# First expert's token slots from one comparison pass, and the selection rounds moved between the weight splits of expert 0

## The reference

```python
aff = jax.nn.softmax((tok @ w_router).astype(jnp.float32), axis=-1)
cap = EC_CAPACITY_FACTOR * N // N_EXPERTS          # 64 of the 512 tokens of a group
gate, idx = lax.top_k(aff.T, cap)
xs = tok[idx]
hid = jax.nn.silu(jnp.einsum('ecd,edf->ecf', xs, w_exp_gate)) * jnp.einsum('ecd,edf->ecf', xs, w_exp_up)
out = jnp.einsum('ecf,efd->ecd', hid, w_exp_down) * gate[..., None].astype(h.dtype)
y = jnp.zeros((N, D), out.dtype).at[idx.reshape(-1)].add(out.reshape(-1, D))
```

## Time and profile before

| | us |
|---|---|
| median of three executions | 2386.59 (2385.63 to 2387.28) |
| the profiled execution, its own time | 2386.68 |
| span of its trace, first to last instruction | 2384.8 |
| TensorE busy in it | 2360.4 |
| VectorE, ScalarE, GpSimd busy | 1624.6, 1488.6, 401.4 |

### The profile page before, as it was taken

The page is one execution under the profiler, slowest core; times in us unless marked ns, Lnnn a source line. Parts: engine busy times, 40 slices in busy tenths (PEclk is TensorE's granted clock), DMA queues, the critical chain, the costliest instruction groups (busy, mean ns, idle before and its releaser), DMA issues.

```text
span 2384.8 us, 33778 instructions
## 1 busy us (share of the span) xinstructions
PE 2360.4 (99%) x11804; PEld 1967.3 (82%) x11804; DVE 1624.6 (68%) x1767; ACT 1488.6 (62%) x1707; POOL 401.4 (17%) x279
## 2 busy tenths in 40 slices
PE   8999999999999999999998999999999999999998
PEld 7888888888888888888885888888888888888886
DVE  5545464634546455455346988888888888888897
ACT  5656564533466465554335777777777777777776
POOL 1533433000053324320002000000000000000000
PEclk9999999999999999999999999999999999999999
DMA  6413321125432224112238999999999999999998
GB/s 189 128 45 100 88 73 67 70 98 204 158 98 83 83 62 126 64 63 80 90 155 334 403 393 382 383 383 381 390 387 393 387 383 383 385 387 376 394 375 326
DMA packets 214395, 557.35 MB, mean 234 GB/s; under 512 B 11968, under 2 KB 93376, under 8 KB 209216
## 3 DMA queue, kind: packets, MB, share of 16 engines
q1 hardware_dynamic: 207280, 530.89, 60.4%
q0 software_dynamic: 7056, 25.69, 3.6%
HBM read 533.47 MB, written 23.07 MB: 233 GB/s over the span
## 4 chain that ended last, share of the span: by engine, by line
PE 97%; DVE 1%; DMA 0%; issue 0%; ACT 0%; POOLq 0%; SPq 0%; DVEq 0%; ACTq 0%
PE bank L1433 44%; PE bank L1073 15%; PE bank L1118 13%; PE bank L1039 7%; PE bank L1062 5%; PE bank L1093 3%; PE bank L1236 2%; PE bank L1479 2%; PE bank L1134 2%; PE bank L1217 1%; PE bank L1156 1%; PE bank L1197 1%; PE bank L1203 1%; PE bank L1160 1%; PE bank L1252 0%
## 5 line engine op out<-in xcount | busy, mean ns | idle before, releaser
L2575 DVE TENSOR_TENSOR m_lo<-m_raw,m_hi 128x2048 fp32r<-128x2048 f32 x380 | 867.4, 2290 | 121.0 <-ACT m_hi L1925 117.4
L1925 ACT ACTIVATE m_hi<-m_raw 128x2048 fp32r<-128x2048 f32 x382 | 733.6, 1921 | 261.5 <-PE bank L1433 256.6
L1433 PE MATMUL bank<-m_hi,xs_hi 128*128 128x512 f32 x1032 | 321.0, 392 | 0.0
L1433 PE MATMUL bank<-m_hi,xs_lo 128*128 128x512 f32 x1032 | 317.9, 389 | 0.0
L1433 PE MATMUL bank<-m_lo,xs_hi 128*128 128x512 f32 x1032 | 317.8, 389 | 0.0
L2063 DVE TENSOR_TENSOR w_lo<-w_raw,w_hi 128x1152 fp32r<-128x1152 f32 (+4 forms) x110 | 145.0, 1344 | 180.1 <-ACT w_hi L1561 180.0
L1433 PEld LDWEIGHTS bank<-m_lo,xs_hi 128*128 128x128 f32 x1032 | 193.7, 188 | 40.5
L1433 PEld LDWEIGHTS bank<-m_hi,xs_lo 128*128 128x128 f32 x1032 | 193.7, 188 | 40.4
L1433 PEld LDWEIGHTS bank<-m_hi,xs_hi 128*128 128x128 f32 x1032 | 191.4, 188 | 38.2 <-DVE xs_lo L2597 0.2
L1073 PE MATMUL bank<-h_hi,w_hi 128*128 128x512 f32 x512 | 203.0, 396 | 0.0
L1073 PE MATMUL bank<-h_lo,w_hi 128*128 128x512 f32 x512 | 199.6, 390 | 0.0
(11 more groups left out here) (292 smaller groups left out, 4239.4 us busy)
## 6 DMA issues: line engine op xcount, KB each, us to landing
m_raw<-in_w_exp_gate SPq DMA_DIRECT2D x128, 1024.0 KB, 8.1
m_raw<-in_w_exp_up SPq DMA_DIRECT2D x128, 1024.0 KB, 7.6
m_raw<-in_w_exp_down SPq DMA_DIRECT2D x128, 1024.0 KB, 7.4
w_raw<-in_w_b SPq DMA_DIRECT2D x66, 512.0 KB, 6.2
w_raw<-in_w_a SPq DMA_DIRECT2D x24, 1024.0 KB, 5.1
w_raw<-in_w_c SPq DMA_DIRECT2D x24, 1024.0 KB, 4.8
w_raw<-in_w_d SPq DMA_DIRECT2D x8, 1024.0 KB, 6.5
xt<-in_x SPq DMA_DIRECT2D x8, 512.0 KB, 7.9
```

The costliest lines, as they stand in the source:

```text
L1433: mm = pe.matmul(ps[:, half, :], a[:, chunk + k, :], v[:, k, 512 * half:512 * (half + 1)], start=first and k == n == 0, stop=last and k == ...
L1925: act.activation(m_hi[slot.slot][:, :, :], m_raw[raw.slot][:, :, :], ACT.Copy)\
L2575: dve.tensor_tensor(m_lo[slot.slot][:, :, :], m_raw[raw.slot][:, :, :], m_hi[slot.slot][:, :, :].bitcast(F32), ALU.subtract)\
```

## The change

1. **First expert's slots.** For expert 0 alone the tokens are no longer taken from the selection rounds. The affinities of expert 0, multiplied by 2^64 (`raised`), are transposed onto all partitions, four tiles of 128 tokens for each group. VectorE then compares each tile with all tokens that can stand ahead of it (`compared`, four SCALAR_TENSOR_TENSOR instructions of 512, 384, 256 and 128 columns, each of which also sums its row), TensorE counts the other side of the comparisons, the difference of both is the token's rank, and an equality with a table of slot numbers marks its slot. TensorE picks token numbers and affinities with these marks. This is done for group 0 inside the closing schedule, for group 1 at its end. The table is loaded into a buffer that is free by then.
2. **The rounds.** The selection rounds, which still make the lists of experts 1 to 15, stand later on VectorE: rounds 0 to 2 while the first rows are gathered, rounds 3 to 5 behind the split of unit 10, rounds 6 and 7 and the merge behind that of unit 15. The filler that went with them is gone, and `WARM_GATHER` is 3 instead of 6.
3. **GpSimd** splits unit 0 alone, behind the issue of the first gather; units 1 and 2 go to VectorE, behind the split of the first rows.
4. **Loading.** SyncE issues three units, and the fourth waits for the rows of the first gather and for the picks. `final_gain` is loaded later.
5. **Order of expert 0.** All its gate and up columns come first (16 units), then all its down columns (8), then the first gate and up columns of expert 1. The loop covers experts 1 to 14.

The core of the diff:

```diff
-WARM_START, WARM_FIRST, WARM_GATHER, WARM_SPLIT, WARM_NORM = 3, 1, 6, 2, 4
-WARM_ROUNDS = {1: 1, 2: 1, 3: 1, 4: 1, 5: 1, 6: 1, 7: 1}
+WARM_START, WARM_FIRST, WARM_GATHER, WARM_SPLIT, WARM_NORM = 3, 1, 3, 2, 4
-EARLY_SPLITS = 2
+POOLED = (0,)
+RAISE = 2.0 ** 64
...
-                ("N", 3), ("k", 2), ("e", 0), ("l", 2), ("L", 3), ("E", 1), ("k", 3), ("e", 1), ("l", 3),
-                ("E", 2), ("E", 3), ("e", 2), ("b", 0), ("e", 3), ("B", 3)]
+                ("N", 3), ("k", 2), ("e", 0), ("l", 2), ("L", 3), ("t", 1, 0), ("E", 1), ("k", 3), ("e", 1), ("l", 3),
+                ("t", 1, 1), ("E", 2), ("E", 3), ("e", 2), ("t", 1, 2), ("e", 3), ("t", 1, 3), ("b", 0), ("B", 3), ("q", 0),
+                ("r", 1, 0), ("r", 1, 1), ("r", 1, 2), ("r", 1, 3), ("d", 3), ("c", 1), ("o", 1), ("q", 1), ("p", 1)]
...
-                if unit.k == RAW_SLOTS - 1:
+                if unit.k == 3:
 
                     sp.wait_ge(s_gather, 16)
+                    sp.wait_ge(s_picked, 2 * NB)
...
+            def compared(of, nth):
+
+                j, cols = NT - 1 - nth, P * (NT - nth)
...
+                dve.scalar_tensor_tensor(beats[j][:, :], ranked[of][:, 0:cols], raised[:, of, j:j + 1], margins[:, T - cols:],
+                                         ALU.subtract, ALU.is_gt, accum_out=row_sum[:, of, j:j + 1]).then_inc(s_beats, 1)
...
+            gate_cols()
+            hidden_transposes(1)
+            up_cols()
+            operand_ready()
+            lists_turned()
+            for j in range(4):
+                use(ps_d, hid_hi, hid_lo, MK * j, j == 0, False)
+                if j == 2:
+                    hidden_transposes(2)
+            operand_ready(1)
+            for j in range(4):
+                if j == 2:
+                    operand_ready()
+                use(ps_d, hid_hi, hid_lo, MK * j, False, j == 3)
+                if j == 2:
+                    token_transposes(32)
```

More of the change, by code:

```diff
@@ L602, in tile_read, with lo_ready @@
             eng.wait_ge(s_proj_free[proj.slot], START + proj.lap + 1)
+        def lo_ready(eng, unit, behind=0):
+            k = unit.k - behind
+            if k in POOLED:
+                eng.wait_ge(s_plo, POOLED.index(k) + 1)
+            else:
+                eng.wait_ge(s_mlo, unit.n(1 - behind - sum(each < k for each in POOLED)))
         def all_stored(eng, count):
@@ L990, in _ @@
             gather(1, 1)
-            with pool.Fori(0, NE - 2) as e:
+            pool.wait_ge(s_mtr, 8)
+            pool.wait_ge(s_gather, 32)
+            gather(2, 2)
+            add(0, 3)
+            with pool.Fori(1, NE - 2) as e:
                 pool.wait_ge(s_mtr, e * 6 + 6)
@@ L1310, in seam_step @@
                     pe.matmul(logits[i], parts[i % 2], fold[:, :], start=True, stop=True).then_inc(s_logit, 1)
+                elif what == "t":
+                    of = arg[0]
+                    if i == 0:
+                        all_read(pe, s_out_free, outs)
+                        all_read(pe, s_proj_free, proj, but=0 if of else 2)
+                    pe.wait_ge(s_raised, of * (1 + i) + 1)
+                    pe.transpose(ranked[of][:, natural(i)], raised[:, of, i:i + 1].to_broadcast([P, P]), ident[:, :])\
+                        .then_inc(s_rows, 1)
+                elif what == "c":
+                    if i == 0:
+                        all_read(pe, s_sc_free, sc)
+                    for j in range(NT - 1, 0, -1):
+                        pe.wait_ge(s_beats, i * NT + NT - j)
+                        for k in range(j):
+                            last = pe.matmul(counts[i], beats[j][:, natural(k)], unit_cols[:, k, :],
+                                             start=j == NT - 1 and k == 0, stop=j == 1)
+                    last.then_inc(s_counts, 1)
+                elif what == "q":
+                    pe.wait_ge(s_hot, 2 * i + 1)
+                    mine = slice(CAP * i, CAP * (i + 1))
+                    for k in range(NT):
+                        for part in range(2):
+                            last = pe.matmul(pick[mine, :], hot_16[:, i, k, :], tokens_16[:, i, k, part:part + 1],
+                                             start=k + part == 0, stop=k + part == NT)
+                    last.then_inc(s_picked, 1)
+                    pe.wait_ge(s_hot, 2 * i + 2)
+                    for k in range(NT):
+                        last = pe.matmul(pick_gate[mine, :], hot[:, i, k, :], raised[:, i, k:k + 1],
+                                         start=k == 0, stop=k == NT - 1)
+                    last.then_inc(s_picked, 1)
                 elif what == "b":
@@ L2039, in _ @@
             per = {"raw": 24, "slot": 24, "unit": 24, "done": 24, "tr": 6, "step": 2}
-            with rolled(act, NE - 1, mt, per) as e:
-                expert(e)
+            with rolled(act, NE - 2, mt, per) as e:
+                expert(e + 1)
             last_expert()
```

284 lines of the change are left out of this document (214 added, 70 removed).

## The result

The changed kernel takes 2391.61 us (median of 17 executions, 2389.16 to 2393.33), the kernel before 2386.52 (17, 2384.83 to 2388.47). The ratio is 1.0021 with a 95% interval of 1.0014 to 1.0027: 5.1 us slower, 6.5 us above the 2385.1 that I forecast and outside my range. The profiled execution of the changed kernel took 2389.88.

What follows compares the result with a forecast made beforehand. TensorE, busy 2360.4 of 2384.8 us, was taken as the bound. An earlier start of -9.0 and stalls of +7.2 gave -1.8, taken as -1.6 with small waits, from 2386.6: 2385.1 us, range 2381.2 to 2389.4.

Steps and rivals of the forecast that it cites:

- -9.0 for the start: First gather's rows land at 1275.4 instead of 1284.4, so expert work begins 9.0 us earlier, at 1278.3.
- +7.2 for the stalls: TensorE waits in expert 0: 3.3 us at unit 11, 1.5 at 16, 0.8 at 17 and 18 together, 1.6 at 20.
- 0.2 us for small waits: Waits of 0.04 us at each unit, counted to turn the sum of -1.8 into -1.6.
- The seam, +1.0: Ahead of the last norms, group 0's four transposes and six small matmuls on TensorE delay everything following by 1.0 us.
- The comparison chain: From last reciprocal at 1264.4 to gather issue at 1271.2; as rival, delayed to 1277.6, +4.8 us or more, 3 in 100.
- "It is not later than the issue": With three weight units beside it, the last store of rows lands no later than the gather's issue at 1271.2.
- The gather itself: The first gather takes 4.2 us (3.4 to 4.9) from issue to rows landed.
- The fourth unit: Issued when rows land, at 1275.4, it arrives 5.3 us later, then one unit per 2.56 us; split in time.
- both rivals on slow weights: Units come every 3.37 us behind the gather: five so, 2388.3 us (12 in 100); twelve or more, 2390.8 (8 in 100).
- "From unit 24 on everything stands as before.": After expert 0's units, the rest of the kernel was to run unchanged, at no cost.
- The clock: TensorE's raised clock might return 2 us late near the gather, moving the start 1 to 2 us.
- the cover of the rounds: Rival: VectorE builds full lead, stalls for rounds shrink from 4.8 to about 0.5 us; 2380.6 us, 17 in 100.

Runs made afterwards that it cites:

- Experiment 1: Changed kernel with the transposes of group 0's raised affinities one tile later in the closing schedule; 2390.33 us, kernel before 2386.75.
- Experiment 6: Changed kernel with weight units 1 and 2 issued only when the last normalised rows are stored; 2391.22 us, kernel before 2387.14.
- Experiment 2: Also written rounds_in_wait: changed kernel with rounds 3 and 4 moved into the gather wait, round 5 ahead of unit 8's split; 2386.58 us, kernel before 2386.75.
- Experiment 11: Idle two-column matmuls added ahead of the loop, 55 to the changed kernel, 64 to 512 to the kernel before; an iteration took 67.96 or 68.05 to 68.06 us.
- experiment 4: Also written filler_4: changed kernel with WARM_GATHER 4 instead of 3, one more filler in the gather wait; 2391.94 us, kernel before 2386.75.
- experiment 5: Changed kernel with the edits of Experiment 1 and Experiment 2 together; 2385.70 us, kernel before 2387.14.
- experiment 10: Kernel before with the fourth weight unit waiting for the first gather's rows and ScalarE's rounding of it behind xs_hi; 2390.37 us, unedited 2386.26.
- padded: Changed kernel with 55 two-column matmuls more behind the gather wait's filler, run once for the loop's pace; 68.05 us for an iteration.
- seven_units: Changed kernel with seven weight units issued ahead of the first gather and the eighth waiting for the rows; 2392.71 us, kernel before 2386.75.

## Why the prediction was wrong

By its own steps, in the order of the sum. The sum was -9.0 for the start and +7.2 for the stalls, -1.6 with 0.2 us for small waits; the profiled pair shows +3.3, and the medians +5.1.

- **The seam, +1.0.** It was +1.43 at the first addition behind the transposes (`xr` at 1233.00 for 1231.57 in the earlier trace rows), and 0.25 more behind the counts. The step counted instructions and left out that the transposes wait for VectorE's `raised`. Experiment 1 shows the wait and its size.
- **The comparison chain** came out at the right place, index at 1269.92 where I had 1270.2, but partly by luck: it began 0.5 us later than I had it (the last reciprocal at 1264.91 for 1264.4) and was 0.8 shorter from there, 5.0 us for 5.8. The four comparisons took 1.96 us where 1.6 had been counted in proportion to their columns. The small matmuls were cheap, as taken (eight picks and their latency 0.58 us), and VectorE's comparison of 512 columns took 0.75 where I had 0.69.
- **"It is not later than the issue"**, the last store of rows. This is the step that failed in the start: the store took 10.12 us with three units beside it, as it had with seven (10.6), and 1.7 us late from the seam it landed at 1271.94. The gather was issued at 1272.99, 1.05 us behind that landing, instead of 1271.2. The kernel before could have warned me: its last store of rows was issued at 1260.14 and landed at 1270.72, so with my own +1.0 and the same 10.6 us the forecast landing is 1271.7, behind the forecast issue. I had taken that fewer units make the store quicker, without a row for it; the units that share the engines with it are the first three, and those had stayed. Experiment 6, with one unit in place of three, shows the sharing: 6.2 us.
- **The gather itself**, 4.2 us, was right (4.21). So work began in effect at 1280.1 where I had 1278.3, -7.2 for -9.0.
- **The fourth unit**: rounding began at 1283.74, 6.5 us behind the rows, where I took 5.3 with 6.2 as the upper end. The bound was too tight. The next unit's rounding began 3.0 us behind it, and from there they came 2.56 us apart, as taken; both rivals on slow weights, with 3.37 us a unit, are wrong.
- **The stalls, 7.2.** Places and releasers were right: unit 11 by VectorE with 3.32 us (forecast 3.3), unit 20 by the hidden operand with 1.41 (1.6), 0.81 at unit 16 (1.5), 0.32 at 18 (0.8 for two). Unit 8, forecast without a wait, had 0.73. But a wait was priced at its idle time alone, and with the restart they are 8.4; 0.5 us more up to unit 40 are not assigned; the two transposes of the lists, which now lie among expert 0's matmuls, are probably a part of them. Experiment 2 takes the largest stall away, and its cost with it.
- **"From unit 24 on everything stands as before."** Wrong by 1.4 us, the loop's pace (14 iterations at 0.10 us). Experiment 11 shows that added idle matmuls ahead of the loop do the same; why is open. Nothing in the profile of the kernel before pointed to it.
- **The clock.** I had it return late or not; it came back in time (1.00 from 1277), and what I had not thought of is that a stall of the forecast's size can drop it again. The profiles of experiments 1, 4 and 6 show it happen behind waits of 3.12, 3.32 and 2.75 us at unit 11. Of the 5.1 us, 1.8 lie between the profiled pair and the medians; that this is their cause fits the mean clocks of the changed kernel's executions (experiment 4) and experiment 2, which took the stall away and gained 5.3 instead of 3.6, though those medians are uncertain by more than the difference; it is not shown directly.

So +1.8 at the start, +1.7 in the stalls and +1.4 in the loop make -1.6 into +3.3. The step that failed at the start is the store's landing, the term of the stalls was sized too small, and the loop was put at nothing. The case that came true was none of my rivals. They took the weights' pace, the cover of the rounds and the comparison chain as what could differ, and none the landing of the store, the price of a stall on TensorE or the loop. The version with both repairs (experiment 5) comes out at -1.4 us where the forecast had -1.5 for a kernel without them; that is within what the measurement can tell from no change.

## What to carry to other kernels

When a long chain is made shorter, look up what else had been finishing under its cover: here a store that took 10 us became the last thing that the gather waited for, and moving it ahead of the weights only moved the wait. Price a stall on TensorE from start to start, not by the idle time, and ask what it does to the clock behind it. Where the work that causes a stall fits into another stretch in which its engine is idle, move it there first. A wait added to one engine's queue must be followed through every engine's list behind it: a gate on a weight load held up the token rows for 6.9 us until ScalarE's order was changed too.

## What the runs showed of the hardware

- The pace of an unchanged loop depended on how many matmuls stood ahead of it in TensorE's program: 67.96 us with 0, 64, 128 and 512 added, 68.05 to 68.06 with 192, 256 and 346.
- A gather of 128 rows of 4 KB took 4.2 to 4.5 us with the queues all but empty (the changed kernel, experiment 10), 7.6 with two weight loads of 1 MB beside it, and 8.0 with four ahead of or beside it. A store of 512 KB took 2.9 us alone, 6.2 with one such load issued ahead of it and 10.1 to 10.6 with three or seven; beside all but the first another store of 512 KB was under way.
- Small matmuls didn't hold TensorE's clock, though they show as busy, and each float32 one is two matmul records in the trace. The 55 added ones of experiment 11 took 0.38 us each, and in 16 us of nothing else the granted clock was 0.50 with TensorE busy all the time (timeline of TensorE, and stretch, of "padded"):

```profile
1275.10 20.98 PE L1501 MATMUL bank<-ident 128*128 128x2 f32 x110
```

```profile
1279.00:1295.00 16.00, 16.00 (x77) 16.00 (x76) 0.00 (x0) 0.00 (x0) 0.00 (x0) 0.50 0.97 379
```

- Long runs of the smallest ones (one column by two, 22 to 26 ns a record) were broken by stretches in which TensorE stood and nothing that the profile shows released it: none with 64 and 128 of them, 3.00 us with 192, 1.26, 3.68 and 0.39 with 256, 4.50 and 1.49 with 512. Whether instructions came too slowly, and whether that has to do with the pace of the loop, no run tells.
- In nine places of seven profiles TensorE stood for 2.75 to 5.82 us at the gathered rows or at unit 11. In eight of them its granted clock fell to 0.5 (1.2 GHz) within the wait or up to 2 us behind it. The ninth is the changed kernel's own 3.32 us, behind which it stayed at 1.00, while filler_4's equal 3.32 was followed by 0.50 in 1316.5 to 1319.5. Behind waits of 1.1 to 1.7 us (the changed kernel, filler_4 and rounds_in_wait at the rows, seven_units at unit 11) it stayed at 1.00.
